# Scores of the second attention in two fp32r passes of stacked halves, with unrotated context keys and queries in four places in turn

## The chip, the cores and the metric

The program runs on one core of a Trainium2 chip, in one launch. The metric is device time in microseconds, the median of several runs. The engines are TensorE (PE; PEld is its loading of weights), VectorE (DVE), ScalarE (ACT), GpSimd (POOL) and SyncE (SP, which here only issues DMAs). Each takes its instructions in the order in which they are written, and they wait for each other by semaphores.

## The reference, cut to what matters

Two layers run over 1024 latent tokens and 256 context tokens of width 1024. The change touches the attention of the second layer (odd_mixer): 12 query heads in 4 groups that share keys and values, width 64, a window of plus and minus 128 tokens beside the whole context, and a learned sink in the softmax.

```python
k_ctx, v_ctx = gqa_keys_values(h_ctx, k_g)            # rmsnorm of keys
q_lat = apply_rope(gqa_queries(h_lat, q_g), cos, sin)
k_lat = apply_rope(k_lat, cos, sin)
...
s_ctx = jnp.einsum('bqkgd,bckd->bkgqc', qi, k_ctx).astype(jnp.float32) * scale
s_win = jnp.einsum('bqkgd,bskd->bkgqs', qi, ki).astype(jnp.float32) * scale
s_win = jnp.where(valid, s_win, NEG_INF)
p = jax.nn.softmax(jnp.concatenate([s_ctx, s_win, sink_col], axis=-1), axis=-1)
```

Context keys have no position, so they are normalized but not rotated; in the kernel before they go through the rotation all the same, with a table that leaves them as they are.

## The kernel before

The stage is heads1(), one block between the projection of queries, keys and values and the output projection. QK1 holds for each group G two tiles of 128 rows: tile 0 has the queries of head j = 2 and the keys, tile 1 the queries of heads j = 0 and 1. Columns 0 to 1023 are latent tokens, 1024 to 1279 context.

Preparing a group takes five **products** w = 0 to 4 (prods): tile 0 in chunks of 512, 512 and 256 columns (c = 2 is the context keys), tile 1 in two of 512. A product goes through ACT's square, PE's norms (one matmul with bones for the sum of squares into bank NB, one with rot1 into bank TB), ACT's inverse (Ln, Exp), and on DVE turn (L2060, q times cos and gain, into t1) and rotated (L2074, L2077, and the multiplications of L2084 that write qa and ka, 64 rows each; semaphore "out"). POOL's cast makes bf16 copies qb and kb of them.

The bf16 copies serve the **maxima**: for each head jj = 0, 1, 2 of a group (j = 2, 0, 1) and query tile qt, PE's maximum (L1908 to L1913) makes scores in banks RB and RB + 1, and DVE's reduce_max (L2095) their largest; the next maximum on PE waits until the one before it is reduced ("mc"). After eight of them DVE's negated and PE's rows (L1923) put the negative maxima in one row, and ACT's row (L1983) copies it to row 64 of qa, where ka has a one, so that the QK matmul subtracts it. The next maximum waits for that copy ("mr").

A **head** n has six pairs u of score units, two of context (512 queries each) and four of window tiles (256 or 384 queries). PE's qk (L1844, fp32, and masks at L1847) makes the units in three banks in turn, ACT's attend (L2005) takes the exponential, PE's pv (L1855) multiplies by values, POOL's add (L1812, L1817) sums the probabilities. For the head before, PE's spread (L1876, L1880) brings sum and sink to all rows in bank NB, in pair u = 1; ACT's inverse_sum (L2012, L2014) inverts, DVE's finish (L2050) writes the output in pair u = 2. ACT's end copies the head's output (L2021) and takes the sink's exponential (L2023).

The order on each engine is written out by hand. A **pair** is a step of 0 to 71 (6 per head, NP_ = 18 per group). In each, PE does qk of the next pair, spread if u = 1, the steps of side 0, pv, the steps of side 1; ACT does the exponentials of the next pair, inverse_sum, then its steps; DVE finish and its steps; POOL casts and add. slots says which steps stand where: product() puts one at pair o + r, o the group's first pair, r = -15, -13, -9, -7, -3, and maxima() starts at r = -8, -2 and 4. What group 0 needs before its first head has the pair UPFRONT; it makes the setup, before the first qk. Banks NB and TB are shared by norms and spread: spread waits for "out" of the norms issued so far, norms for "out" of the product before.

## Time and profile before

| | |
|---|---|
| median of 3 runs | 3388.43 us (3385.56 to 3391.74) |
| the profiled execution's own time | 3388.43 us |
| its span | 3386.7 us |
| PE busy | 3165.7 us (93%) |
| DVE, ACT, POOL busy | 1582.6, 1015.1, 464.9 us |
| heads1, from its start to its last copies | about 2215 to 2533 us |
| QK matmuls of the stage | 288 records, two for each fp32 matmul |

Busy time is summed over an engine's instructions; PE's ends are modelled, so the distance of two starts says more about the cost of a piece than its length. A row of a timeline merges equal neighbours (x4 is four of them), and what stands in brackets is the engine's idle time before it and who ended it.

### The profile page before, as it was taken

How to read it: one execution, taken by the hardware profiler on the slowest of the kernel's cores; microseconds unless marked ns; L12 is line 12 of the kernel's file. 1: busy time of each engine (PE TensorE's matmuls, PEld its weight loads, DVE VectorE, ACT ScalarE, POOL GpSimd, SP SyncE). 2: the span in 40 equal slices, each digit the busy share in tenths (PEclk: the TensorE clock that was granted, in tenths of full speed). 3: DMA queues.
4: the chain of work that ended last, by engine and by line, in shares of the span. 5: the costliest groups of instructions: out<-in, count | busy, mean ns of one | idle time of the engine just before them, and what ended most of it. 6: DMA issues, size and time to landing. Idle time of an engine off the chain costs nothing. (4 is left out here: it accounts for less than half of the span.)

```text
span 3386.7 us, 37587 instructions
## 1 busy us (share of the span) xinstructions
PE 3165.7 (93%) x14242; PEld 2176.1 (64%) x14242; DVE 1582.6 (47%) x1955; ACT 1015.1 (30%) x1363; POOL 464.9 (14%) x367
## 2 busy tenths in 40 slices
PE   5987999999897999999999978879989899999998
PEld 2552333333386888888888856734438688888887
DVE  4123544554425454444444553355533555555554
ACT  3014555555413111111111131025542312221221
POOL 0002555555400000000000000035540000000000
PEclk8987999999998999999999989989999999999999
DMA  9800000000201111111111001000001211111111
GB/s 381 326 36 17 4 3 2 3 3 0 85 27 46 37 37 37 37 37 37 37 37 37 31 13 44 31 16 1 1 13 37 70 44 43 62 43 40 47 62 50
DMA packets 34911, 162.27 MB, mean 48 GB/s; under 512 B 3890, under 2 KB 6706, under 8 KB 24755
## 3 DMA queue, kind: packets, MB, share of 16 engines
q1 hardware_dynamic: 34834, 161.24, 13.3%
q8 instruction: 49, 0.80, 0.1%
q14 instruction: 28, 0.22, 0.0%
HBM read 157.03 MB, written 4.19 MB: 48 GB/s over the span
## 5 line engine op out<-in xcount | busy, mean ns | idle before, releaser
L716 PE MATMUL PS<-f_uh,f_Wh 128*128 128x512 f32 (+1 forms) x1760 | 483.4, 372 | 26.0 <-DVE f_ul L453 25.2
L716 PE MATMUL PS<-f_ul,f_Wh 128*128 128x512 f32 (+1 forms) x1760 | 481.4, 371 | 0.0
L716 PE MATMUL PS<-f_uh,f_Wl 128*128 128x512 f32 (+1 forms) x1760 | 481.3, 371 | 0.0
L866 DVE SCALAR_TENSOR_TENSOR X<-PS,mod,X 128x512 f32<-128x512 f32 (+1 forms) x440 | 305.9, 697 | 308.2 <-PE PS L716 308.2
L716 PEld LDWEIGHTS PS<-f_uh,f_Wh 128*128 128x128 f32 x1760 | 308.2, 188 | 89.6 <-issue 19.4
L716 PE MATMUL PS<-f_gh,f_WDh 128*128 128x512 f32 (+1 forms) x880 | 330.4, 375 | 19.5 <-DVE f_gl L852 17.2
L716 PEld LDWEIGHTS PS<-f_ul,f_Wh 128*128 128x128 f32 x1760 | 308.5, 188 | 59.1
L716 PEld LDWEIGHTS PS<-f_uh,f_Wl 128*128 128x128 f32 x1760 | 308.3, 188 | 59.1
L716 PE MATMUL PS<-f_gl,f_WDh 128*128 128x512 f32 (+1 forms) x880 | 325.3, 370 | 0.0
L716 PE MATMUL PS<-f_gh,f_WDl 128*128 128x512 f32 (+1 forms) x880 | 324.6, 369 | 0.0
L835 DVE SCALAR_TENSOR_TENSOR part<-PS,part,part 128x1023 f32<-128x1023 f32 (+1 forms) x132 | 130.0, 1012 | 329.9 <-ACT part L771 329.9
L771 ACT ACTIVATE part<-PS,part 128x1280 f32<-128x1280 f32 (+1 forms) x88 | 115.7, 1315 | 420.6 <-PE PS L716 420.6
L1214 POOL TENSOR_TENSOR X<-X 128x1024 f32<-128x1024 f32 x96 | 227.9, 2374 | 78.1 <-ACT X L1429 78.1
L777 ACT ACTIVATE part<-part 128x1280 f32<-128x1280 f32 (+1 forms) x44 | 51.4, 1169 | 621.0 <-DVE part L841 621.0
L1239 PE MATMUL PS<-part,part 97*128 97x512 f32 x480 | 232.9, 608 | 0.7 <-ACT part L1420 0.7
L716 PEld LDWEIGHTS PS<-f_gh,f_WDh 128*128 128x128 f32 x880 | 166.1, 189 | 54.3 <-issue 17.9
L1429 ACT ACTIVATE X<-PS 128x512 f32<-128x512 f32 x252 | 146.1, 593 | 179.7 <-PE PS L1239 154.1
L716 PEld LDWEIGHTS PS<-f_gl,f_WDh 128*128 128x128 f32 x880 | 166.4, 189 | 27.9
L716 PEld LDWEIGHTS PS<-f_gh,f_WDl 128*128 128x128 f32 x880 | 166.3, 189 | 28.1
L1785 POOL MEMSET part<- 64x1280 f32 x2 | 2.3, 1161 | 1310.8 <-POOLq L134 1310.8
L1528 DVE TENSOR_REDUCE part<-PS 128x1 f32<-128x512 f32 (+1 forms) x312 | 162.9, 580 | 30.2 <-PE PS L1325 29.0
L823 DVE TENSOR_TENSOR f_Wl<-part,f_Wh 128x1024 fp32r<-128x1024 f32 x88 | 107.5, 1222 | 105.6 <-ACT f_Wh L761 105.6
(255 smaller groups left out, 4283.0 us busy)
## 6 DMA issues: line engine op xcount, KB each, us to landing
part<-in_mod_w SPq DMA_DIRECT2D x48, 1024.0 KB, 7.4
part<-in_w_up SPq DMA_DIRECT2D x88, 512.0 KB, 3.5
part<-in_w_down SPq DMA_DIRECT2D x22, 1024.0 KB, 5.6
part<-in_w_out SPq DMA_DIRECT2D x16, 512.0 KB, 3.5
X<-in_xT SPq DMA_DIRECT2D x4, 1280.0 KB, 9.8
X<-in_xT SPq DMA_DIRECT2D x1, 5120.0 KB, 16.1
part<-in_wqk SPq DMA_DIRECT2D x8, 512.0 KB, 3.5
out<-X SPq DMA_DIRECT2D x16, 256.0 KB, 2.0
```

Of the source, the lines that this page charges most:

```text
L716: mm = pe.matmul(ps(bank + c, hi - lo), w_, x_[:, lo:hi], start=f_, stop=l_)
L771: act.activation((cg, cv)[kind][:, :], psv(UPB[kind]), ACT.Identity, scale=cw[:, ds(f, 1), 1], bias=cw[:, ds(f, 1), 3]).then_inc(s["cen"], 1)
L777: act.activation(sg[:, :], cg[:, :], ACT.Silu).then_inc(s["silu"], 1)
L823: dve.tensor_tensor(Wl[place % 2][:, :, :], W[place % 2][:, :, :], Wh[place % 2][:, :, :].bitcast(F32), ALU.subtract).then_inc(s["lo"], 1)
L835: op = dve.scalar_tensor_tensor(out=x[:, lo + 1:hi], in0=h[:, lo:hi - 1], scalar=cw[:, ds(f, 1), 0], in1=x[:, lo + 1:hi], op0=ALU.mult, op ...
L866: dve.scalar_tensor_tensor(out=X[:, m, lo:hi], in0=ps(DNB[r % 2], hi - lo), scalar=moda(layer, 5, m, 0 if lo < SEQ else 1), in1=X[:, m, lo ...
L1214: op = pool.tensor_tensor(ac[:, 0:SEQ], ac[:, 0:SEQ], p[:, :], ALU.add)
L1239: mm = pe.matmul(ps(i % 3, BANK), ka[b][0:97, u * P:(u + 1) * P], qa[b][0:97, n * BANK:(n + 1) * BANK], start=True, stop=True)
L1429: act.activation(pr[u % 3][:, i % 2 * BANK:i % 2 * BANK + BANK], ps(i % 3, BANK), ACT.Exp, scale=A_SCALE).then_inc(s["P"], 1)
L1528: dve.reduce_max(mc[:, r:r + 1], ps(RB + c, hi - lo), AX_X).then_inc(s["mc"], 1)
L1785: pool.memset(ka[b][64:P, :], 0.0).then_inc(s["zero"], 1)
```

## The change

Queries and keys get fp32r tiles. qh holds the high half of a query (rounded to fp32r) in rows 0 to 63 and again in rows 64 to 127, ql the low half (the value less the high half) in rows 0 to 63, with the row of maxima in row 64 and the sink's exponential in row 96. ks holds the low half of a key in rows 0 to 63 and the high half in rows 64 to 127, kh the high half and the row of ones. A unit of QK is two matmuls into one bank: ks with qh, and kh with ql.

The product ends in t1 (one multiplication of 128 rows); a new step "hi" on ACT (high) copies t1 to the high places, and a new step "lo" on DVE (low) subtracts. Both stand one pair after the rotation, POOL's cast waits for "hi", and t1 is free for the next product after "lo". Context keys (c = 2) have neither turn nor rot matmul. Queries have four places in turn, by head, in place of two sets of three. The products stand at r = -15, -13, -12, -6, -3, and the upfront ones are interleaved (upfront). The table of the rotation comes in two loads without its context columns, and PE no longer waits for it; es, osb, lnr and sq lie elsewhere.

```diff
@@ -1681,22 +1681,28 @@
...
-                return big(part[0] - n, *shape)
-            qa = [[take(SEQ) for _ in range(C_GROUP)] for _ in range(2)]
-            ka = [take(T) for _ in range(2)]
-            pr = [take(2, BANK) for _ in range(3)]
-            osb = take(BANK)
-            acc = [take(SEQ) for _ in range(2)]
-            rope = take(2, T)
-            qb = [take(SEQ // 2).bitcast(BF16) for _ in range(C_GROUP)]
-            kb = [take(T // 2).bitcast(BF16) for _ in range(2)]
...
+                return part[0] - n
+
+            def halves(kind, n, size):
+
+                return [place(f"h1_{kind}{b}", take(size), size) for b in range(n)]
+
+            def plain(*shape):
+                return big(take(*shape), *shape)
+
+            QS = 4
+            qh, ql = halves("qh", QS, SEQ), halves("ql", QS, SEQ)
+            ks, kh = halves("ks", 2, T), halves("kh", 2, T)
...
+            rope = [plain(SEQ), MIX1[:, 5, :]]
...
+            sq = [QK1[:, 4 * b + 1:4 * b + 4:2, SEQ:T] for b in range(2)]
+            t1, lnb, osb, lnr = [X[:, 2 * b:2 * b + 2, SEQ:T] for b in range(4)]
...
@@ -1720,9 +1726,18 @@
...
                 at(pair - 1, 1 if pair > 1 else 0, "sq", G, w)
+                at(pair - 1, 1 if pair > 1 else 0, "tn", G, w)
                 at(pair, 0, "nt", G, w)
                 at(pair, 1, "ro", G, w)
+                at(pair + 1, 0, "hi", G, w)
                 at(pair + 1, 0, "ca", G, w)
+                at(pair + 1, 1, "lo", G, w)
...
+            def upfront(n):
...
+                for kind, w in [("sq", 0), ("nt", 0)] + [(kind, w + d) for w in range(n) for kind, d in (
+                        ("sq", 1), ("tn", 0), ("ro", 0), ("nt", 1), ("hi", 0), ("lo", 0), ("ca", 0)) if w + d < n]:
+                    at(UPFRONT, 0, kind, 0, w)
...
@@ -1735,8 +1750,12 @@
             def plan(G):
 
                 o = NP_ * G
-                for w, r in enumerate((-15, -13, -9, -7, -3)):
-                    product(o + r if G else 1 if w == 4 else UPFRONT - 1, G, w)
+                if G == 0:
+                    upfront(NW - 1)
+                    product(1, G, NW - 1)
+                else:
+                    for w, r in enumerate((-15, -13, -12, -6, -3)):
+                        product(o + r, G, w)
...
@@ -1769,6 +1788,21 @@
...
+                def queries(G, j):
+
+                    return (C_GROUP * G + JS.index(j)) % QS
+
+                def operands(G, w):
+
+                    t_, c = prods[w]
+                    b, lo, hi = G % 2, *CH[c]
+                    j = 2 if t_ == 0 else 0
+                    low, high = slice(0, 64), slice(64, P)
+                    out = [] if c == 2 else [(low, qh[queries(G, j)], low, high, ql[queries(G, j)])]
+                    if t_ == 0:
+                        return out + [(high, ks[b], high, None, kh[b])]
+                    return out + [(high, qh[queries(G, 1)], high, low, ql[queries(G, 1)])]
+
                 def halved(x, m):
                     return x[:, 0:m // CTX, :]
 
@@ -1777,31 +1811,31 @@
...
-                    sp.dma_start(rope, a["rope1"]).then_inc(s["tab"], 16)
+                    for t_ in range(2):
+                        sp.dma_start(rope[t_], a["rope1"][:, t_, 0:SEQ]).then_inc(s["tab"], 16)
...
-                        pool.wait_ge(s["out"], NW * G + w + 1)
+                        pool.wait_ge(s["hi"], NW * G + w + 1)
                         at_least(pool, "mx", 24 * (G - 1) + (8 if t_ == 0 else 24))
                         if t_ == 0:
                             if c < 2:
-                                pool.tensor_copy(qb[2][0:64, lo:hi], qa[b][2][0:64, lo:hi])
-                            op = pool.tensor_copy(kb[b][0:64, lo:hi], ka[b][0:64, lo:hi])
+                                pool.tensor_copy(qb[2][0:64, lo:hi], qh[queries(G, 2)][0:64, lo:hi].bitcast(F32))
+                            op = pool.tensor_copy(kb[b][0:64, lo:hi], kh[b][0:64, lo:hi].bitcast(F32))
                         else:
-                            pool.tensor_copy(qb[0][0:64, lo:hi], qa[b][0][0:64, lo:hi])
-                            op = pool.tensor_copy(qb[1][0:64, lo:hi], qa[b][1][0:64, lo:hi])
+                            for j in range(2):
+                                op = pool.tensor_copy(qb[j][0:64, lo:hi], qh[queries(G, j)][0:64, lo:hi].bitcast(F32))
                         op.then_inc(s["cast"], 1)
...
@@ -1839,10 +1873,14 @@
                             at_least(pe, "P", i - 2)
                             if u == 0 and c == 0:
                                 pe.wait_ge(s["mr"], n + 1)
+                                pe.wait_ge(s["lo"], NW * G + (3 if j == 2 else NW))
...
-                            mm = pe.matmul(ps(i % 3, w), ka[G % 2][:, kt * P:(kt + 1) * P],
-                                           qa[G % 2][j][:, q0 * P:q1 * P], start=True, stop=not last)
+                            q = queries(G, j)
+                            pe.matmul(ps(i % 3, w), ks[G % 2][:, kt * P:(kt + 1) * P], qh[q][:, q0 * P:q1 * P],
+                                      start=True, stop=False)
+                            mm = pe.matmul(ps(i % 3, w), kh[G % 2][:, kt * P:(kt + 1) * P], ql[q][:, q0 * P:q1 * P],
+                                           start=False, stop=not last)
...
@@ -1890,9 +1928,12 @@
...
                         nb, tb = banks(G, w)
-                        pe.matmul(ps(nb, hi - lo), bones, sq[q % 2][:, :hi - lo], start=True, stop=True)
-                        pe.matmul(ps(tb, hi - lo), rot1[:, 1 - t_, :], QK1[:, 2 * G + t_, lo:hi],
-                                  start=True, stop=True).then_inc(s["nt"], 1)
+                        m = hi - lo
+                        mm = pe.matmul(in_halves(ps(nb, m)), bones, halved(sq[q % 2], m), start=True, stop=True)
+                        if c < 2:
+                            mm = pe.matmul(ps(tb, m), rot1[:, 1 - t_, :], QK1[:, 2 * G + t_, lo:hi],
+                                           start=True, stop=True)
+                        mm.then_inc(s["nt"], 1)
...
@@ -1976,12 +2016,27 @@
...
+                    def high(G, w):
...
+                        act.wait_ge(s["out"], q + 1)
...
+                        for rows_, first, own, other, second in operands(G, w):
+                            x = halved(t1[rows_], m)
+                            act.activation(in_halves(first[own, lo:hi]), x, ACT.Copy)
+                            if other:
+                                op = act.activation(in_halves(first[other, lo:hi]), x, ACT.Copy)
+                            else:
+                                op = act.activation(in_halves(second[0:64, lo:hi]), x, ACT.Copy)
+                        op.then_inc(s["hi"], 1)
...
@@ -2056,34 +2114,48 @@
...
-                        at_least(dve, "out", NW * G + w)
+                        if c == 2:
+                            return
+                        at_least(dve, "lo", NW * G + w)
...
-                                                 in1=in_halves(rope[:, 0, lo:hi]), op0=ALU.mult, op1=ALU.mult)\
+                                                 in1=in_halves(rope[0][:, lo:hi]), op0=ALU.mult, op1=ALU.mult)\
...
                     def rotated(G, w):
-                        b = G % 2
...
                         q = NW * G + w
+                        r = (NW - 1) * G + w - (w > 2)
+                        nb, tb = banks(G, w)
+                        norm_ = in_halves(ps(nb, m))
+                        if c == 2:
+                            at_least(dve, "lo", q)
+                            dve.wait_ge(s["rinv"], q + 1)
+                            dve.scalar_tensor_tensor(out=halved(t1, m), in0=in_halves(QK1[:, 2 * G + t_, lo:hi]),
...
+                            return
...
-                        dve.tensor_tensor(T_, T_, rope[:, 1, lo:hi], ALU.mult).then_inc(s["ts"], 1)
-                        dve.wait_ge(s["ts"], q + 1)
-                        dve.wait_ge(s["t1"], q + 1)
+                        dve.tensor_tensor(T_, T_, rope[1][:, lo:hi], ALU.mult).then_inc(s["ts"], 1)
+                        dve.wait_ge(s["ts"], r + 1)
+                        dve.wait_ge(s["t1"], r + 1)
                         dve.tensor_tensor(halved(t1, m), halved(t1, m), in_halves(T_), ALU.add).then_inc(s["ta"], 1)
-                        dve.wait_ge(s["ta"], q + 1)
+                        dve.wait_ge(s["ta"], r + 1)
                         dve.wait_ge(s["rinv"], q + 1)
-                        dsts = [qa[b][2] if c < 2 else None, ka[b]] if t_ == 0 else [qa[b][0], qa[b][1]]
-                        for r, dst in enumerate(dsts):
-                            if dst is not None:
-                                rows_ = slice(64 * r, 64 * r + 64)
-                                op = dve.tensor_tensor(in_halves(dst[0:64, lo:hi]), halved(t1[rows_], m),
-                                                       in_halves(ps(nb, m, rows_)), ALU.mult)
-                        op.then_inc(s["out"], 1)
+                        dve.tensor_tensor(halved(t1, m), halved(t1, m), norm_, ALU.mult).then_inc(s["out"], 1)
...
+                    def low(G, w):
...
+                        dve.wait_ge(s["hi"], NW * G + w + 1)
+                        for rows_, first, own, other, second in operands(G, w):
+                            out = second[0:64, lo:hi] if other else first[0:64, lo:hi]
+                            op = dve.tensor_tensor(in_halves(out), halved(t1[rows_], m),
+                                                   in_halves(first[own, lo:hi].bitcast(F32)), ALU.subtract)
+                        op.then_inc(s["lo"], 1)
...
```

## Rows read from the trace of the kernel before

**Rows 1.** The page: span, and busy time of each engine.

```profile
span 3386.7 us, 37587 instructions
...
PE 3165.7 (93%) x14242; PEld 2176.1 (64%) x14242; DVE 1582.6 (47%) x1955; ACT 1015.1 (30%) x1363; POOL 464.9 (14%) x367
```

**Rows 2.** Busy time by stretch, engine by engine, with granted clock (PEclk).

```profile
2214.90:2249.80 34.90, 18.53 (x54) 7.80 (x54) 23.26 (x35) 7.80 (x13) 14.48 (x17) 0.66 0.11 38
2249.80:2533.00 283.20, 273.89 (x1370) 124.17 (x1370) 146.04 (x198) 145.07 (x251) 136.37 (x137) 0.99 0.00 1
```

**Rows 3.** Timeline of ACT: Ln of product 2, groups two apart.

```profile
2297.11 0.47 ACT L1973 ACTIVATE X<-PS,eps 128x256 f32<-128x256 f32 x1 [0.43 <-PE PS L1894]
...
2439.13 0.47 ACT L1973 ACTIVATE X<-PS,eps 128x256 f32<-128x256 f32 x1 [0.43 <-PE PS L1894]
```

**Rows 4.** Timeline of PE: start, length, engine, line, operation, tiles, shape, count.

```profile
2301.65 1.94 PE L1844 MATMUL PS<-part,part 128*128 128x512 f32 x4
2303.43 1.02 PE L1893 MATMUL PS<-part,cst 128*128 128x512 f32 x2
...
2305.14 0.27 PE L1908 MATMUL PS<-part,part 128*128 128x256 bf16 x1
...
2314.31 1.08 PE L1855 MATMUL PS<-part,part 128*64 128x512 f32 x4
2315.34 0.27 PE L1908 MATMUL PS<-part,part 128*128 128x256 bf16 x1
...
2315.72 0.86 PE L1844 MATMUL PS<-part,part 128*128 128x384 f32 x2
```

**Rows 5.** Timeline of the projection before heads1, on fp32r operands.

```profile
2082.17 0.63 PE L555 MATMUL PS<-u1h,qk_wh 128*128 128x512 f32 x2
...
2082.64 0.63 PE L555 MATMUL PS<-u1l,qk_wh 128*128 128x512 f32 x2
```

**Rows 6.** Groups by line and shape: count, busy us, mean ns, idle before.

```profile
L2095 DVE TENSOR_REDUCE part<-PS 128x1 f32<-128x640 f32 x72 | 59.1, 824 | 76.8 <-PE PS L1913 76.7
...
L2005 ACT ACTIVATE part<-PS 128x384 f32<-128x384 f32 x72 | 35.4, 491 | 44.7 <-PE PS L1847 43.4 <-POOL part L1817 1.1
...
L2084 DVE TENSOR_TENSOR part<-X,PS 64x512 f32<-64x512 f32 x32 | 21.9, 684 | 1.1 <-DVE X L2077 0.4
...
L2023 ACT ACTIVATE part<-part,sml 1x1024 f32<-1x1024 f32 x12 | 13.7, 1143 | 0.3
...
L1973 ACT ACTIVATE X<-PS,eps 128x512 f32<-128x512 f32 x16 | 11.0, 688 | 34.0 <-PE PS L1894 34.0
...
L1963 ACT ACTIVATE part<-part 128x512 f32<-128x512 f32 x16 | 9.9, 621 | 5.4 <-PEq L134 5.4
```

**Rows 7.** Timeline of the setup: memsets, first norms, first reductions, first QK.

```profile
2215.14 2.89 DVE L2117 MEMSET part<- 64x640 uint32 x5 [1.26 <-PEq L134]
...
2220.48 2.07 PE L1893 MATMUL PS<-part,cst 128*128 128x512 f32 x2 [7.92 <-DMA part<-in_rope]
...
2224.30 0.70 DVE L2074 TENSOR_TENSOR PS<-PS,part 128x512 f32<-128x512 f32 x1 [3.01 <-PE PS L1894]
...
2241.09 2.97 DVE L2095 TENSOR_REDUCE part<-PS 128x1 f32<-128x512 f32 x4
...
2249.85 5.37 PE L1844 MATMUL PS<-part,part 128*128 128x512 f32 x8 [1.20 <-ACT part L1983]
```

**Rows 8.** L2060 (min/median/max ns), and one of it beside POOL's adds.

```profile
L2060 DVE SCALAR_TENSOR_TENSOR X<-part,sml,part x20: 485/777/1498, 2220.5 to 2460.9; 128x512 f32<-128x512 f32 x16, 128x256 f32<-128x256 f32 x4
...
2300.02 3.54 POOL L1817 TENSOR_TENSOR part<-part,part 128x384 f32<-128x384 f32 x3
...
2301.20 1.50 DVE L2060 SCALAR_TENSOR_TENSOR X<-part,sml,part 128x512 f32<-128x512 f32 x1
```

**Rows 9.** Timeline of PE: maximum 4 of head 1 in group 0.

```profile
2265.12 0.28 PE L1908 MATMUL PS<-part,part 128*128 128x256 bf16 x1 [1.76 <-POOL part L1804]
```

**Rows 10.** Busy time of PE and granted clock by stretch, setup.

```profile
2242.00:2246.00 4.00, 3.29 (x20) 0.69 0.00 0
```

More of the change, by code:

```diff
@@ L1753, in heads1 @@
                      ("tab", "one", "zero", "pad", "s8", "S", "P", "PV", "sq", "nt", "ln", "rinv",
-                      "t1", "ts", "ta", "out", "cast", "mx", "mc", "mn", "mrow", "mr", "o", "es",
+                      "t1", "ts", "ta", "out", "hi", "lo", "cast", "mx", "mc", "mn", "mrow", "mr", "o", "es",
                       "ad", "bc", "lnr", "rs", "fin")}
@@ L1784, in _ @@
                     for b in range(2):
[L1785 removed]
+                        pool.memset(kh[b][64:P, :].bitcast(F32), 0.0).then_inc(s["zero"], 1)
                         pool.wait_ge(s["zero"], b + 1)
[L1787 to L1790 removed]
+                        pool.memset(kh[b][64:65, :].bitcast(F32), 1.0).then_inc(s["one"], 1)
+                    for x in ql:
+                        pool.memset(x[64:P, :].bitcast(F32), 0.0).then_inc(s["one"], 1)
                     def cast(G, w):
@@ L1879, in spread @@
                         for c in range(2):
-                            mm = pe.matmul(ps(NB, BANK, slice(64 * c, 64 * c + 64)), ones[64:65, 0:64],
-                                           es[64:65, c * BANK:(c + 1) * BANK], start=False, stop=True)
+                            mm = pe.matmul(ps(NB, BANK, slice(64 * c, 64 * c + 64)), ones[96:97, 0:64],
+                                           ql[n % QS][96:97, c * BANK:(c + 1) * BANK].bitcast(F32), start=False, stop=True)
                         mm.then_inc(s["bc"], 1)
@@ L1991, in side @@
                                 inverse(*what)
+                            elif kind == "hi":
+                                high(*what)
                             elif kind == "row":
@@ L2020, in end @@
                         at_least(act, "fin", n)
-                        act.activation(osb, ps(OB, BANK), ACT.Copy).then_inc(s["o"], 1)
+                        act.activation(osb, in_halves(ps(OB, BANK)), ACT.Copy).then_inc(s["o"], 1)
                         at_least(act, "bc", n)
-                        act.activation(es[64:65, :], qa[G % 2][j][64:65, :], ACT.Exp, scale=C_SCALE,
+                        act.activation(ql[n % QS][96:97, :], ql[n % QS][64:65, :].bitcast(F32), ACT.Exp, scale=C_SCALE,
                                        bias=sml[64:65, W_SINK + h:W_SINK + h + 1]).then_inc(s["es"], 1)
@@ L2110, in side @@
                                 rotated(*what)
+                            elif kind == "lo":
+                                low(*what)
                             elif kind == "max":
```

54 lines of the change are left out of this document (28 added, 26 removed).

## The prediction

> **What bounds the kernel now.** I read the page first: TensorE (PE) is busy 3165.7 of a span of 3386.7 us, so a change counts where it takes PE work away or makes PE wait [rows 1]. The profiled execution's own time is 3388.43 us, 1.7 above its span, and equals the median of the three runs, so the sum below is made against 3388.4. The shown runs lie 6.2 us apart; 0.2% is 6.8 us, about what a measurement can tell from no change.
>
> Then the busy time by stretch, cut at the two borders of heads1. A setup of 34.9 us (2214.9 to 2249.8) runs at a mean granted clock of 0.66 with PE busy half the time; then come 283.2 us in which PE is busy 273.9, at a clock of 0.99, against 146 for DVE, 145 for ACT and 136 for POOL [rows 2]. So the setup is a chain of latencies, and the rest is PE's alone. The row of Ln on 256 columns (once in a group, product 2) comes at 2297.11 and, two groups later, at 2439.13: a group of 18 pairs takes 71.0 us [rows 3]. Inside a pair PE starts its next piece where the last ends. The reader should read the starts, not the durations (the ends are modelled): two QK units of 512 take 1.78 us (2301.65 to 2303.43), a norms step of 512 1.71, a PV 1.03, one maximum 0.38 [rows 4].
>
> **What is taken away: fp32 QK.** A unit of 512 columns costs 1.78/2 = 0.89 us. The new passes run on fp32r operands, which this trace has in the projection before: two matmuls of 512 in 0.47 us (2082.17 to 2082.64), each with its own weights [rows 5]. A unit is now two such passes, 0.47. A head has 4 units of 512, 6 of 384, 2 of 256, in all 4864 columns or 9.5 units of 512; twelve heads, 114. At 0.42 each that is 48 us; part of 0.89 is the edge between instructions, so I take 46. Context keys (c = 2) no longer have the rot matmul: half of 1.71 for 512 columns, so 0.43 for 256, four times, 1.7. Together **-47.5**. Bounds: -44 if the edges stay whole, -48.
>
> **What is added.** Each product now ends in a step "hi" on ACT (four copies of 64x512; two of 64x256 for c = 2) and a step "lo" on DVE (two subtractions; one). The nearest copy of ACT from SBUF takes 0.62 us and, back to back, some 0.53 apart: "hi" is 2.1 us. The nearest DVE row with its shape is the old write of the result, 64x512 at 0.68 [rows 6]; two are 1.4, and one multiplication of 128x512 takes the place of two of 64x512, so DVE's "ro" is 0.7 shorter. But the subtraction has both inputs in SBUF, as the rotation's first operation (L2060) has, and that takes from 0.485 to 1.50 us, 1.50 while POOL runs its adds [rows 8]. POOL's casts now wait for the same "hi" as the subtractions, so they run at the same moment. I take 2.0 us for "lo" (1.4 alone; 2.8 if each is doubled).
> The Trainium skill says, on the page "SBUF — State Buffer", section "Who interferes with whom", that a DVE instruction with two SBUF inputs contends with a GpSimd instruction that reads SBUF and that one holds the other up whole. The spread of L2060 agrees; by the rule an add of 384 columns could hold a subtraction up for all of its own time, and each "lo" would cost more than my 2.0.
>
> In busy time all of this fits: per group ACT gets 4 x 2.1 + 0.8 = 9 us more on 145/4 = 36, DVE nearly the same as before, where PE would have 71.0 - 11.8 = 59. On average nobody replaces PE. The order of the queues is another matter. "hi" stands on ACT between the exponentials; "lo" stands on DVE *before* the reduction of a maximum in two slots of a group, and PE may not issue maximum m + 1 before the reduction of m is done. And spread shares banks with the norms, so it waits for "out" of the last norms issued, and the norms of products 2 and 3 now stand one pair before a spread.
>
> **Stalls in one group**, PE against the chain, pairs counted from the group's first:
> - Pair 13 (product 3). After spread, ACT does the two steps of inverse_sum (1.3, by the Ln and Exp of a product), then "hi" 2.1, DVE "lo" 2.0, then the reduction 0.82; with handovers 6.5. PE meanwhile has maximum 0.38, PV 1.18, maximum 0.38, QK 1.0 = 3.0. It waits **3.5**.
> - Pair 16 (product 4). From the pair's start ACT has 1.1 left, a copy of a row (1x1024, as the sink's row, 1.14), exponentials 1.0 (2 x 0.49) [rows 6], "hi" 2.1, then "lo" 2.0, reduction 0.8: 7.1. PE reaches its next maximum at 4.1 (QK 1.0, two passes of 512 for each of two units, or of 384 with masks; wait for the row copy and maximum 0.8; PV 0.95; maximum 0.38; QK 1.0). **3.0**.
> - Pair 6 (products 1 and 2), before the spread of pair 7. ACT is at Ln and Exp of product 1 until 0.5 us into the pair, then at a square (0.3), the end of the head (copy 0.6, sink 1.1) and the exponentials (1.0) until 3.5; "hi" of product 1 to 5.6; "lo" to 7.7; DVE's last multiplication of product 2 0.6 more, 8.3. PE reaches the spread at 4.5 (QK 0.98, maximum, norms 0.43 with a wait, PV, maximum, QK 0.65). **3.8**.
> - Small ones: spread of pair 13 behind "out" of product 3, 0.95; square of product 1 behind "hi" of product 0, 0.5; norms 2 behind "out" of product 1, 0.5; three row copies against a shorter QK, 1.0.
>
> Sum 13.3 per group. It is more than the 11.8 that QK and rot give back, so a group with products would take 59.2 + 13.3 = 72.5 against 71.0. Three groups have such a cycle (products of groups 1 to 3), 40 us; the first already has about 2 of idle in it. **+38**. Behind the last product 15 pairs run free and keep their gain, less **1** for row copies.
>
> **Setup.** Before, the first norms wait for the table until 2220.48 and are seen at 2224.30 (3.8 us, twice the 1.71 of the fast clock); the reductions start at 2241.09 and QK at 2249.85 [rows 7]. Now PE waits only for the memsets, which end at 2218.0, so the first norms are seen near 2222. But upfront() interleaves, and DVE and ACT are both in order: "lo" 0 waits for "hi" 0, which stands behind Ln and Exp of product 1 (square and norms: 2222 + 1.3 + 0.6 + 3.8 = 2227.7; done 2229.0); "hi" 0 to 2231.2, "lo" to 2233, rotation 1 to 2236, "hi" 1 to 2238.4; the square of product 3 only then, its norms at the low clock to 2243, Ln and Exp to 2244.2, "hi" 2 to 2245, rotation 3 to 2248.6, "hi" 3 to 2250.9, "lo" 3 to 2252.5. The reductions of all eight maxima stand behind it: 2252.5 against 2241.09, **+11.5**. Bounds +8 (clock high for the norms, no contention) and +14.
> - Product 4 of group 0, norms in pair 1: maximum 4 needs its cast, already a wait of 1.76 us on POOL [rows 9]; now "hi" (2.1) and a shorter QK come before it: **+3** (2 to 4).
> - Clock. In the setup, behind idle, PE was granted 0.69 over 2242 to 2246 us though busy 3.29 of the 4, so a good part of it at 1.2 GHz [rows 10]. Waits of 3 us in a stream may bring the same; I take **+3** for nine of them.
> The rest has cover: two smaller loads in place of one, memsets of POOL (four places in place of six), the lower place of t1 and osb.
>
> Sum: -47.5 + 38 + 1 + 11.5 + 3 + 3 = +9; 3388.4 + 9 = **3397 us**.
>
> **Rivals.**
> - *The waits stay hidden* (other side). If "lo" is never in front of a reduction that PE needs, because "hi" starts before the point that I give it, groups run at 59 us: 3388.4 - 47.5 + 11.5 + 3 + 1 = 3356. For it: ACT and DVE are busy only half the time [rows 2]. It decides at the 3.0 us that PE has between spread and the next-but-one maximum: "hi", "lo" and reduction alone are 4.9. Chance 0.19. Half the stalls, 3377: 0.12.
> - *The clock falls in the waits.* Each of nine long waits is followed by a stretch of about 4 us at 1.2 GHz [rows 10], costing some 1.5 to 2 us: 9 x 1.7 = 15 in place of 3: 3409. Against it: with PE busy 82% of a group the clock could stay. Chance 0.17. The Trainium skill (page "TensorE: Matmul & The Clock Gate", section "What's actually happening") has the throttled state as the default that activity releases; that speaks for this rival.
> - *The passes are not at the fp32r rate here* (the change doesn't do what it says): at 0.89 per unit again, the stalls shrink to those of spreads and setup: 3388.4 + 15 + some 10 = 3413. Nothing in rows 5 speaks for it. Chance 0.04.
> - My forecast, stalls that eat the gain, 3390 to 3404: 0.48.
>
> **The numbers.** Slower by over 0.2% (above 3395.2): two thirds of the forecast 0.31, the clock 0.15, the rate 0.04 = 0.50. Same: rest of the forecast and an edge of the clock case, 0.20. Faster: 0.30. The range must go down into the rival of hidden waits: 3364 to 3413 leaves out about 0.15 below and 0.04 above. The likeliest case's own range is 3388 to 3406 (stalls 11 to 16 per group, setup 8 to 14).
>
> **What would show it.** QK passes of 512 about 0.235 us apart; fp32r copies and subtractions on ACT and DVE, 64x512 at 0.6 and 0.7 to 1.3; PE idle in heads1 of some 40 to 50 us, released by DVE's reduction twice a group and by DVE's last product before the spread of pair 7; the group period near 72 us in place of 71.0; first QK some 61 us behind 2200 in place of 49.85. If the group period is near 60, my ledger of the queues is wrong; if the period is 72 with stalls elsewhere, only their places are.

## The result, and the profile after

| | |
|---|---|
| the changed kernel | 3435.77 us, median of 4 runs |
| the kernel before, beside it | 3387.78 us (3385.56 to 3391.74, 4 runs) |
| ratio | 1.0131 [1.0107, 1.0155]: slower by 48 us by the medians, 44 by the ratio |
| profiled execution | 3435.32 us, span 3433.5 us, against 3388.43 and 3386.7 |

One of the four runs, of 4083.2 us, was disturbed; the ratio leaves it out. The other three are 3426.07, 3435.32 and 3436.22 us, so what an experiment gains on the changed kernel is 1 to 4 us more by the medians than by the ratios; where that matters, the stretch of the heads in the two traces is given too. The forecast was 3397 (3364 to 3413): slower is right, by five times the amount. The page has PE busy for 11 us less than before, and still the span is 46.8 us longer [rows 1].

```profile
span 3433.5 us, 37657 instructions
...
PE 3154.6 (92%) x14234; PEld 2177.8 (63%) x14234; DVE 1603.5 (47%) x1963; ACT 1053.4 (31%) x1435; POOL 473.6 (14%) x365
```

Next the windows of the changed kernel, cut at the first memset of POOL, the first QK and the first matmul of the output projection ([rows 2] ended 8 us ahead of that); the last row is one cycle of the groups, from Ln on 256 columns to the next one.

```profile
2215.17:2261.85 46.68, 18.74 (x52) 7.64 (x53) 24.33 (x36) 16.25 (x27) 15.25 (x15) 0.59 0.07 23
2261.85:2586.49 324.64, 260.60 (x1364) 125.02 (x1365) 168.61 (x209) 178.43 (x313) 144.20 (x137) 0.87 0.01 4
2387.19:2469.92 82.73, 67.64 (x354) 32.69 (x354) 47.96 (x59) 47.52 (x84) 38.33 (x36) 0.90 0.00 1
```

The kernel before, with the same cuts:

```profile
2214.95:2249.85 34.90, 18.53 (x54) 7.83 (x55) 23.26 (x35) 7.80 (x13) 14.48 (x17) 0.66 0.11 38
2249.85:2541.38 291.53, 273.90 (x1371) 124.17 (x1371) 149.24 (x202) 148.66 (x255) 136.37 (x137) 0.98 0.01 5
```

The setup is 11.8 us longer, the stretch of the heads 33.1, all the rest 1.9. This cycle takes 82.7 us and the one before it 85.7, where both took 71.0 [rows 3]. PE's granted clock in the heads fell from 0.98 to 0.87. These are PE's waits of over 0.4 us in one cycle, from the timeline:

```profile
2389.47 1.08 PE L1914 MATMUL PS<-part,cst 128*64 128x512 f32 x4 [2.55 <-DVE X L2136]
...
2412.67 1.08 PE L1914 MATMUL PS<-part,cst 128*64 128x512 f32 x4 [0.73 <-DVE X L2148]
...
2423.93 0.37 PE L1949 MATMUL PS<-part,part 128*128 128x256 bf16 x1 [6.12 <-issue]
...
2438.88 0.37 PE L1949 MATMUL PS<-part,part 128*128 128x256 bf16 x1 [3.51 <-issue]
...
2460.88 1.13 PE L1932 MATMUL PS<-part,cst 128*128 128x512 f32 x2 [0.57 <-ACT part L2003]
...
2466.76 0.67 PE L1932 MATMUL PS<-part,cst 128*128 128x256 f32 x2 [1.50 <-issue]
```

They sum to 15.0 us; the ledger had 13.3. The two long ones are the two maxima behind a "lo"; there the view names no releaser ("issue"), so we must look at what DVE did. Around the 6.12, all engines:

```profile
2417.87 0.63 ACT L2031 ACTIVATE h_qh<-X 64x512 fp32r<-64x512 f32 x1
2418.53 4.57 DVE L2156 TENSOR_TENSOR h_ql<-X,h_qh 64x512 fp32r<-64x512 f32 x2 [2.42 <-ACT h_qh L2031]
2418.62 1.62 POOL L1838 CAST part<-h_qh 64x512 bf16<-64x512 f32 x2 [13.32 <-issue]
2420.21 2.33 POOL L1846 TENSOR_TENSOR part<-part,part 128x1024 f32<-128x1024 f32 x1
2422.63 0.87 ACT L2062 ACTIVATE part<-PS 128x384 f32<-128x384 f32 x2 [4.13 <-issue]
...
2423.02 0.81 DVE L2167 TENSOR_REDUCE part<-PS 128x1 f32<-128x640 f32 x1
```

The two subtractions take 4.57 us for both; the forecast had 2.0. They start together with POOL's casts, which were waiting for the same "hi", and run into POOL's add, which had stood ready behind the casts. The add also lets go the exponentials of the next pair, which wait 4.13. Taken one by one, the first subtraction lasts 0.68 us and the second, from 2419.23, 3.87: it ends 0.56 behind the add. By this pair alone the contention could be the whole story; the experiments ask how much of the 48 us it is, how much is the order of the queues, how much the passes and how much the clock.

### The profile page after: what moved, and what is told of

Same layout as the page of the kernel before. It is cut to its first block and busy times, and to the rows that moved or that the text cites. A ratio compares the mean times of both kernels' runs of the same rounds, so it can differ in the third digit from the quotient of the medians.

```text
span 3433.5 us, 37657 instructions
## 1 busy us (share of the span) xinstructions
PE 3154.6 (92%) x14234; PEld 2177.8 (63%) x14234; DVE 1603.5 (47%) x1963; ACT 1053.4 (31%) x1435; POOL 473.6 (14%) x365
## 6 DMA issues: line engine op xcount, KB each, us to landing
X<-in_xT SPq DMA_DIRECT2D x1, 5120.0 KB, 16.1
```

## The experiments

Times are medians, each beside the kernel before on the same chip; the ratio is to that kernel.

**1. One wait moved: POOL's cast behind "lo".** In groups 1 to 3 the casts can no longer run beside the subtractions.

```diff
-                        pool.wait_ge(s["hi"], NW * G + w + 1)
+                        pool.wait_ge(s["lo" if G else "hi"], NW * G + w + 1)
```

> The changed kernel, but POOL's cast of the groups after the first waits for the subtractions (lo) in place of the copies (hi), so that neither the casts nor the add of 1024 columns behind them can run beside the subtractions. Theory 1 (the two subtractions of pair 13 take 4.57 us because POOL's instructions hold them up): they fall to 1.4, the wait of PE in pair 14 falls from 6.12 to about 3.0 us in each of three groups, and with less of the low clock behind it the run gets 9 to 15 us shorter, 3421 to 3427. Rival (the length comes from something else in the subtraction, such as its output type or its two inputs alone): the subtractions stay above 3 us and the time stays within 3 us.

3427.89 us (3426.12 to 3429.65), 1.0113 [1.0096, 1.013]. The same place in this kernel:

```profile
2409.44 1.38 DVE L2156 TENSOR_TENSOR h_ql<-X,h_qh 64x512 fp32r<-64x512 f32 x2 [2.42 <-ACT h_qh L2031]
...
2410.94 1.16 POOL L1838 CAST part<-h_qh 64x512 bf16<-64x512 f32 x2 [13.22 <-issue]
...
2412.07 2.34 POOL L1846 TENSOR_TENSOR part<-part,part 128x1024 f32<-128x1024 f32 x1
...
2414.49 0.87 ACT L2062 ACTIVATE part<-PS 128x384 f32<-128x384 f32 x2 [5.09 <-issue]
```

Nothing but POOL's start is different, and the pair of subtractions is down from 4.57 to 1.38: the contention is shown. The maximum now waits 2.94 instead of 6.12. But POOL's add comes no earlier, the exponentials wait 5.09, and the next QK waits for them. So only 8 us came back (6 by the ratios; the heads take 320.94 against 324.64), less than the 9 to 15 expected.

**2. The other order on DVE: "lo" behind the reductions** of its pair, for products 3 and 4.

```diff
-                at(pair + 1, 1, "lo", G, w)
+                if lo:
+                    at(pair + 1, 1, "lo", G, w)
...
-                        product(o + r, G, w)
+                        product(o + r, G, w, w < 3)
...
+                for w, r in ((3, -6), (4, -3)):
+                    if G:
+                        at(o + r + 1, 1, "lo", G, w)
```

> The changed kernel, but for products 3 and 4 of groups 1 to 3 the subtractions stand on DVE behind the reduction of the maximum in the same slot, not ahead of it. Theory 1 (PE waits in pairs 14 and 17 because that reduction is queued behind the subtractions): the waits of 6.1 and 3.5 us go, 29 us in three groups; theory 2 (each long wait is followed by a stretch at 1.2 GHz): another 8 to 15 us come back with it, in all 3391 to 3400. If the clock falls for another reason (a group has too little work for PE in any case) only the waits come back, 3405. Rival to both: the wait moves to the next maximum and the time stays above 3420.

3418.07 us (3416.14 to 3421.18), 1.0085 [1.0068, 1.0102]: a miss, by 18 us and more. The maxima no longer wait, and a QK does:

```profile
2334.31 4.56 DVE L2160 TENSOR_TENSOR h_ql<-X,h_qh 64x512 fp32r<-64x512 f32 x2 [0.92 <-ACT h_qh L2035]
2334.39 1.62 POOL L1842 CAST part<-h_qh 64x512 bf16<-64x512 f32 x2 [13.35 <-issue]
2335.98 2.33 POOL L1850 TENSOR_TENSOR part<-part,part 128x1024 f32<-128x1024 f32 x1
2338.40 0.87 ACT L2066 ACTIVATE part<-PS 128x384 f32<-128x384 f32 x2 [4.12 <-issue]
...
2338.94 0.69 PE L1884 MATMUL PS<-h_qh,h_ks 128*128 128x384 f32 x1 [3.76 <-ACT part L2066]
```

POOL has the cast ahead of the add, and sat 13.35 us idle for it, the last 9 with the add's data at hand (ACT's exponentials of that pair end at 2325.17). The expectation had looked at DVE's queue alone; the same product blocks two queues.

**3. The old places** of the products, all else as changed.

```diff
-                    for w, r in enumerate((-15, -13, -12, -6, -3)):
+                    for w, r in enumerate((-15, -13, -9, -7, -3)):
```

> The changed kernel with the products at the places of the kernel before (-15, -13, -9, -7, -3). Theory 1 (spread waits in pairs 7 and 13 because the norms of products 2 and 3 stand one pair ahead of it): the waits of 2.55, 1.50 and 0.73 us before norms 2 and the spreads go, 14 us in three groups, but product 3's subtractions stand in pair 12, behind no spread, so the 6.1 us wait gets shorter too, to some 3: 3405 to 3418. Rival (the waits are set by the amount of work of ACT, whatever the places): within 5 us of 3436.

3433.76 us (3433.23 to 3435.88), 1.0128 [1.0111, 1.0145]: no difference from the changed kernel, as the rival had it, and the expectation is a miss by 16 us. The waits have other places (4.74, 3.50, 2.76, 2.11 for POOL's cast of product 2, 1.23), and a cycle takes 83.4 and 83.9. The new places are not the cause, and do not help either. That the amount of ACT's work sets the waits, as the rival says, is not shown by it: experiment 6 takes the longest of them away with the same work.

**4. The passes alone.** The kernel before, its queries and keys in fp32r tiles and each unit as two fp32r matmuls of the same operands: no low halves, no "hi", no "lo". It leaves out the low half and counts the high one twice.

```diff
-                            mm = pe.matmul(ps(i % 3, w), ka[G % 2][:, kt * P:(kt + 1) * P],
-                                           qa[G % 2][j][:, q0 * P:q1 * P], start=True, stop=not last)
+                            for f_ in (True, False):
+                                mm = pe.matmul(ps(i % 3, w), ka[G % 2][:, kt * P:(kt + 1) * P],
+                                               qa[G % 2][j][:, q0 * P:q1 * P], start=f_, stop=not (f_ or last))
```

> The kernel before with one edit: qa and ka are fp32r tiles, and a QK unit is two fp32r matmuls of the same two operands in place of one in fp32; the scores come out doubled and there is no low half. No step of the halves on ACT or DVE. It prices the passes alone. Forecast: 44 to 48 us shorter than the kernel before, 3340 to 3344, if PE stays what the stage waits for. Rival (the other engines' chains at once take up what PE gives, even without the halves): less than 30 us shorter, above 3358.

3355.26 us (3353.66 to 3359.35), 0.9898 [0.9882, 0.9915]. That is 34.4 us less than before, a gain, but smaller than both 46 and the expectation. The timeline of the changed kernel shows one part of why; a pair of units there:

```profile
2320.32 0.48 PE L1880 MATMUL PS<-h_qh,h_ks 128*128 128x512 f32 x1
2320.64 0.39 PE L1882 MATMUL PS<-h_ql,h_kh 128*128 128x512 f32 x1
2320.87 0.40 PE L1880 MATMUL PS<-h_qh,h_ks 128*128 128x512 f32 x1
2321.11 0.39 PE L1882 MATMUL PS<-h_ql,h_kh 128*128 128x512 f32 x1
2321.48 0.27 PE L1949 MATMUL PS<-part,part 128*128 128x256 bf16 x1
```

Inside the run a pass takes the 0.23 to 0.24 that was forecast. The first takes 0.32, and behind the last the next maximum starts 0.37 later: 1.16 for the pair of units, where 0.94 was counted (1.03 where an fp32 matmul follows). Pairs of 384 with their masks take 1.21 to 1.26 (2317.44 to 2318.70, for one), where 1.63 less 0.63 was counted, 1.00. The pairs of experiment 4 take the same times. Set against the kernel before, with the same neighbours, a pair of 512 is 0.6 to 0.8 us shorter, where 0.84 was counted, and a pair of 384 is 0.40 to 0.57 shorter, where 0.63 was. Over 24 pairs of 512, 36 of 384 and 12 of 256 that makes some 39 of the 48 us. The other part is waits: in the heads of experiment 4 PE is busy 36.7 us less and waits 5.4 us more. The stretch of the projection from which the price came [rows 5] is one long run, without such edges.

**5. The casts one pair later**, behind "lo" (all but product 2's, which keeps its place).

```diff
-                at(pair + 1, 0, "ca", G, w)
+                at(pair + (2 if G and w != 2 else 1), 0, "ca", G, w)
...
-                        pool.wait_ge(s["hi"], NW * G + w + 1)
+                        pool.wait_ge(s["lo" if G and w != 2 else "hi"], NW * G + w + 1)
```

> The changed kernel with POOL's casts of groups 1 to 3 one pair later (two pairs behind the norms, but product 2's at its old pair) and behind the subtractions. In the changed kernel the cast of pair 13 stands on POOL before the add of that pair and waits for the copies (hi), so the add of 1024 columns ends 4.1 us after ACT is ready for the next exponentials, and it runs beside the subtractions. Theory 1 (POOL's queue and the lock with DVE make the wait of pair 14): subtractions 1.4 us unless an add meets them, PE's wait in pair 14 at most 3 us, ACT's wait for POOL there gone; 3418 to 3424, a few us better than the run in which the cast waits for the subtractions in its old place (3427.9). Rival (that wait is DVE's queue alone): within 3 us of 3427.9.

3418.27 us (3416.55 to 3421.56), 1.0086 [1.007, 1.0103]. As expected: the QK waits of experiment 1 are gone, the maxima still wait up to 2.94 and 2.64.

**6. Both edits**: 5 and 2 together.

> The same, and the subtractions of products 3 and 4 behind the reduction in their slot. Both causes of the waits in pairs 14 and 17 are away, so these waits (6.1 and 3.5 us in three groups) should be gone and not return as waits for exponentials, as they did in part in the run with the reductions alone (3.76 us behind ACT, which was behind POOL). What is left are the waits before norms 2 and the spreads, 4.8 us a group. Forecast 3395 to 3404. Rival (ACT is too full in any order, so PE waits elsewhere): above 3410.

3393.83 us (3389.85 to 3399.3, 10 runs), 1.0018 [1.0009, 1.0028]. That is 1 us below the expected range. Each edit alone gave 17 to 18 us, the two give 42 (in the heads of the traces 16.4, 13.0 and 39.1): with either one the other queue still held PE up. The longest wait left in a cycle is 2.75, of the spread for DVE's last step of product 2.

**7. New places** on top of 6: products 2 and 3 elsewhere, away from that spread.

```diff
-                    for w, r in enumerate((-15, -13, -12, -6, -3)):
+                    for w, r in enumerate((-15, -13, -10, -7, -3)):
```

> The same, with the products at -15, -13, -10, -7, -3: product 2 three pairs and product 3 two pairs ahead of a spread. The waits before norms 2 and the spreads go too, 4.8 us a group and what the clock gives back: 3378 to 3390, that is about the kernel before, because the setup (+12 us) and the larger wait for the first group's cast (+2.5) stay. Rival: as above, above 3395.

3375.93 us (3371.01 to 3381.83, 8 runs), 0.9967 [0.9955, 0.9979]: 2 us below the expected range, and faster than the kernel before by 12 us, with the whole change in it. Its windows, cut as above:

```profile
2213.04:2259.64 46.60, 18.67 (x52) 7.64 (x53) 24.32 (x36) 16.24 (x27) 15.24 (x15) 0.59 0.07 23
2259.64:2527.29 267.65, 238.24 (x1364) 116.86 (x1365) 153.55 (x209) 176.73 (x313) 139.03 (x137) 0.96 0.02 5
2369.75:2434.64 64.89, 61.25 (x356) 29.95 (x358) 43.16 (x59) 46.88 (x85) 35.96 (x36) 1.00 0.00 1
```

The reader should compare PE's busy time: the same 1364 matmuls took 260.60 us in the changed kernel and take 238.24 here. The work is the same; the clock is not (0.87 and 0.96, and in the cycle 0.90 and 1.00). This puts a price of 22.4 us on the clock, 6.4 of it in each cycle. The waits of this cycle are 0.57, 0.77, 1.02 and 0.41. Its subtractions, by form, against those of the changed kernel's cycle in the fence behind it:

```profile
L2160 DVE TENSOR_TENSOR h_ql<-X,h_qh 64x512 fp32r<-64x512 f32 x6 | 4.1, 684 | 3.6 <-ACT h_kh L2037 1.8 <-ACT h_qh L2035 1.8
```

```profile
L2156 DVE TENSOR_TENSOR h_ql<-X,h_qh 64x512 fp32r<-64x512 f32 x6 | 8.2, 1360 | 5.2 <-ACT h_qh L2031 4.5 <-ACT h_kh L2033 0.5
```

**8. The clock by itself.** The changed kernel, with matmuls that nobody reads put into the two long waits of groups 1 to 3: five of fp32 ahead of the maximum of pair 14, three ahead of that of pair 17. DVE, ACT and POOL keep their order and their contention.

```diff
                     def maximum(G, jj, qt):
                         pe.wait_ge(s["cast"], NW * G + (3 if jj == 0 else 4 if qt < 4 else 5))
+                        if G and (jj, qt) == (0, 7):
+                            fill(5)
+                        if G and (jj, qt) == (1, 2):
+                            fill(3)
```

> The changed kernel, with matmuls that nobody reads (fp32, 512 columns, into bank TB) put on PE where it waits: five before maximum 7 of head 0 (pair 14), three before maximum 2 of head 1 (pair 17), in groups 1 to 3. They take 4.3 and 2.6 us of waits of 6.1 and 3.5 us, so they cost nothing if the waits stay. Theory 2 (the waits let the granted clock fall, and PE then works at 1.2 GHz for some us while there is work): the granted clock stays at 1.00 behind both waits and the run gets 8 to 14 us shorter, 3422 to 3428. Rival (the low clock has another cause, or costs nothing because PE waits again later): within 3 us of 3436, or longer.

3422.99 us (3419.07 to 3426.61), 1.0103 [1.0086, 1.0121]: more work for PE, and 13 us less by the medians (9.5 by the two ratios; 9.4 in the heads by the traces, 315.24 against 324.64). The granted clock behind the wait of pair 14, in windows of 2 us, first of the changed kernel:

```profile
2417.00:2419.00 2.00, 0.81 (x7) 0.48 (x6) 0.47 (x1) 1.48 (x3) 0.38 (x1) 1.00 0.00 0
2419.00:2421.00 2.00, 0.00 (x0) 0.00 (x0) 1.99 (x2) 0.00 (x0) 2.00 (x3) 1.00 0.00 0
2421.00:2423.00 2.00, 0.00 (x0) 0.00 (x0) 2.00 (x1) 0.37 (x1) 1.86 (x2) 0.68 0.00 0
2423.00:2425.00 2.00, 1.07 (x5) 0.58 (x7) 1.96 (x4) 1.13 (x3) 1.78 (x3) 0.50 0.00 0
2425.00:2427.00 2.00, 2.00 (x9) 1.09 (x6) 1.94 (x3) 0.03 (x1) 1.63 (x2) 0.50 0.00 0
2427.00:2429.00 2.00, 2.00 (x6) 0.96 (x6) 0.40 (x2) 0.95 (x2) 0.00 (x0) 0.61 0.00 0
2429.00:2431.00 2.00, 2.00 (x12) 0.63 (x11) 0.90 (x2) 0.90 (x2) 0.00 (x0) 1.00 0.00 0
```

and of the kernel with the filler, whose maximum comes at 2419.74:

```profile
2419.00:2421.00 2.00, 1.84 (x11) 0.71 (x9) 1.96 (x3) 0.98 (x2) 1.78 (x3) 1.00 0.00 0
2421.00:2423.00 2.00, 2.00 (x11) 1.13 (x10) 1.94 (x3) 0.94 (x2) 1.49 (x2) 1.00 0.04 8
2423.00:2425.00 2.00, 2.00 (x14) 0.62 (x12) 1.44 (x4) 1.18 (x2) 0.00 (x0) 1.00 0.01 4
```

Behind the idle wait the clock is at its lower level, 1.2 GHz (0.50), until past 2427; behind the filled one it stays at 2.4 GHz. Six filled waits gave 9.4 us, about 1.6 each. Not every low stretch went: in group 1 the maximum of pair 14 still waited 1.73 us behind its filler, and the clock was low again from 2339 to past 2342; in the cycle shown it was at 0.50 over 2412 to 2414, ahead of the filler and behind the spread's wait of 0.74.

The two long waits are not the only ones with a slow stretch behind them. In the changed kernel the spreads of pair 7 wait 2.00 us in the first of the three groups and 2.55 in the others, and behind each PE works without a pause at the lower level:

```profile
2305.50:2312.00 6.50, 6.50 (x18) 1.34 (x19) 0.82 (x1) 2.03 (x4) 0.74 (x2) 0.51 0.00 0
2391.50:2397.50 6.00, 6.00 (x23) 2.73 (x22) 2.64 (x4) 2.52 (x5) 3.14 (x3) 0.50 0.00 0
2473.50:2479.50 6.00, 6.00 (x18) 1.88 (x18) 1.27 (x2) 2.03 (x4) 1.84 (x2) 0.50 0.00 0
```

Half of that time, 3 us each and 9 in all, is what the lower level costs there, by an estimate from these rows. By the same estimate the low stretches behind the six long waits cost 14 us, of which the filler gave 9.4 back.

**9. The setup by itself.** The changed kernel, with the steps of the first group written out in another order and a second rotation buffer for its products 1 and 3.

```diff
-                for kind, w in [("sq", 0), ("nt", 0)] + [(kind, w + d) for w in range(n) for kind, d in (
-                        ("sq", 1), ("tn", 0), ("ro", 0), ("nt", 1), ("hi", 0), ("lo", 0), ("ca", 0)) if w + d < n]:
-                    at(UPFRONT, 0, kind, 0, w)
+                for step in ("sq0 nt0 sq1 tn0 ro0 tn1 hi0 nt1 lo0 ca0 ro1 sq2 nt2 sq3 ro2 hi1 lo1 ca1 tn3 hi2 lo2 ca2 "
+                             "nt3 ro3 hi3 lo3 ca3").split():
+                    at(UPFRONT, 0, step[:2], 0, int(step[2]))
```

> The changed kernel with the first group's preparation written out anew: the two heads' chains are taken further apart so that products 2 and 3 are not cast before products 0 and 1 have their halves, and products 1 and 3 of that group have a second rotation buffer. Nothing else moves. Theory (the time to the first score is a term of its own, worth its length once): the first score, now at 2261.85, comes some 10 us earlier, near 2251 to 2252, the groups stay at 82 to 86 us, and the whole takes 3424 to 3427. Rival (the early start is lost again in group 0, whose casts come no earlier, or in a lower clock): the first score comes early, but the time stays above 3431.

3424.48 us (3423.59 to 3424.96), 1.0107 [1.009, 1.0124]: 11.3 us less. The setup takes 37.19 us in place of 46.68, and the heads 324.86 in place of 324.64. The new order and the second buffer came together; which of them gave the 9.5 us was not tried.

**10. The setup in the better version**: 7 and 9 together.

> The version with casts one pair later, the low half behind the maxima and places -15, -13, -10, -7, -3 (3375.9 us, first score at 2259.64), with the new order of the first group's preparation as well. Theory: the two gains add, since one lies ahead of the first score and the other in the groups: 3363 to 3368. Rival: with TensorE waiting little in the groups, the early start meets group 0's casts sooner and its wait on GpSimd (4.24 us in the changed kernel) grows by as much: 3372 or more.

3371.23 us (3367.26 to 3373.07), 0.9948 [0.9931, 0.9965]. The setup is shorter by the same 9.4 us, the time by 4.7 (6.4 by the ratios), between the two expectations. From the first QK to the norms of product 2 of group 1, 3.3 us more pass than in experiment 7 (47.83 against 44.52). It is not the rival's wait: that is 4.24 in both, and the others differ by 0.03 at most. It is the clock: the same 185 matmuls keep PE busy 39.03 us at a mean clock of 0.84, against 35.75 at 0.89. Why the low clock falls so much longer there (0.71 over 2273 to 2281, where 7 had 1.00 over 2280 to 2286) is open.

**11. Fewer early maxima**, on top of 10: those that need product 4's cast come a pair later.

```diff
-            EARLY = [(0, 0), (0, 1), (1, 0), (1, 1), (2, 0), (2, 1), (3, 0), (4, 0)]
+            EARLY = [(0, 0), (0, 1), (1, 0), (1, 1), (3, 0), (3, 0), (3, 1), (4, 0)]
```

> The same, and of the maxima of the first group those that need product 4's cast come one pair later. Theory: the wait of TensorE on GpSimd's cast (4.24 us at 2276.75 in the changed kernel) goes down by 2 to 4 us, and the time with it, to 3360 to 3364. Rival: the wait comes back one pair later, as a wait for the same cast, and the time stays within 1 us of the version without this edit.

3371.11 us (3369.72 to 3372.42), 0.9949 [0.9932, 0.9965]: no difference. The wait for POOL went from 4.24 to 2.96 us, and the two after it from 0.55 and 0.83 to 1.90 and 2.22: the rival, as far as the view tells, which names no releaser for the last two.

**12. A single pass**: experiment 4 without the second matmul of a unit. The low half's product is left out wholly.

> The kernel before with its scores from a single pass in fp32r instead of two (3355.3 us with two): the high half of the queries alone, the low half's product left out wholly, so this prices one pass and is no version of the kernel. A second pass of the same weights took 0.235 us per 512 columns. Theory (TensorE sets the time and the second passes cost what they last): 114 of them take 26.8 us, so 3327 to 3332. Rival (other engines have become the bound of the groups by then, at 62.5 us): the gain stays under 15 us, so 3340 or more, and new waits on VectorE or ScalarE stand ahead of the scores.

3348.14 us (3346.03 to 3350.86), 0.9884 [0.9867, 0.99]. Half of QK's columns are gone, and it is 7 us, not 27 (9.7 in the heads of the traces, where PE is busy 22.6 us less and waits 13.0 more). Cycles of 4 and of this kernel:

```profile
2355.38:2418.08 62.70, 60.63 (x358) 30.16 (x360) 41.30 (x58) 36.86 (x66) 34.91 (x36) 1.00 0.00 1
```

```profile
2354.15:2414.16 60.01, 54.41 (x322) 25.26 (x324) 40.48 (x58) 36.43 (x66) 34.86 (x36) 1.00 0.00 1
```

PE works 6.2 us less and waits 3.5 us more in a cycle, though DVE, ACT and POOL are busy two thirds of it at most. The new waits stand ahead of the maxima, not of the scores, and the view names no releaser for them. That a cycle of this order is bound near 60 us by its chains from one engine to the next is read from this, not tried. The gain of faster passes was, by the times, nearly used up at two.

## Why the prediction was right or wrong

The table sets the terms of the sum against what the profiled executions measured. The terms of the heads go from the kernel before over experiment 4, which has the passes and nothing else, to the changed kernel: the stretch takes 291.53, 260.18 and 324.64 us, of which PE is busy 273.90, 237.16 and 260.60.

| term | forecast | measured | from |
|---|---|---|---|
| passes and rot | -47.5 | -31.4 | 260.18 less 291.53 (without rot) |
| waits in the heads, the cast's and the row copies among them | +38 + 3 + 1 | +41.0 | not busy: 64.0 less 23.0 |
| clock | +3 | +23.4 | busy: 260.60 less 237.16; 22.4 against experiment 7 |
| setup | +11.5 | +11.8 | 46.68 less 34.90 |
| outside the stage | 0 | +1.9 | the rest of the span |
| all | +9 | +46.8 | spans 3433.5 and 3386.7 |

- **Passes: direction right, size wrong.** The price of a pass, 0.235, came true inside a run of passes. The step that failed is "I take 46": 2 us were put down for all edges, while every pair of 512 or 384 gives 0.06 to 0.23 less than counted, some 9 us in all. The bound nearer to zero, -44, was still too large. PE was busy 36.7 us less in experiment 4, and 5.4 of it came back there as waits, which the term had at nothing.
- **The ledger of waits: right in sum by luck, wrong in its entries.** 15.0 us in a cycle for 13.3 forecast, and +41.0 in the heads for +42. The wait behind product 3, which shows in pair 14, is 6.12 and not 3.5, by "lo" (4.57 for 2.0) and "hi" (2.53 from 2415.97 to 2418.50, for 2.1). Pair 17 (3.51 for 3.0) and the spread of pair 13 (0.73 for 0.95) are close. Norms 2 wait three times what was put down (1.50 for 0.5). The spread of pair 7 came smaller (2.55 for 3.8), and the row copies (1.0) left no wait over 0.4. The errors cancelled.
- **"lo" at 2.0.** The range ended at 2.8; it took 4.57 beside casts and add, 2.25 beside the casts of product 4, and 1.38 where neither ran beside it. The text had said in so many words that casts and subtractions run at the same moment, and then took a value near the middle. The Trainium skill, page "SBUF — State Buffer", section "Who interferes with whom", says that a DVE instruction with two inputs in SBUF contends with a GpSimd instruction that reads SBUF, and that the port pair they share is locked by one of them at a time. The trace agrees: the second subtraction lasts 3.87 us and ends 0.56 behind POOL's add (2.33).
- **What the ledger lacked**: POOL's own queue. The casts wait for "hi", the add of the pair before stands behind them, and the exponentials wait for the add. In the changed kernel this hides behind the maximum's wait; experiment 2 brought it out.
- **The clock: the rival, and larger.** The forecast took +3, its rival 15 for nine long waits at 1.7 us each. Experiment 8 measures 1.6 per filled wait, near the rival's 1.7; but nine waits of it are 14, and the heads lost 22.4. The rest lies behind the third kind of the nine, the spread of pair 7: at least 9 us by the rows in experiment 8. So the rival had the right nine places, and too low a price for a third of them. Experiment 7, which has no wait over 1.02 in a cycle, has none of these stretches; experiment 6, with the spread's wait still at 2.75, has two (from 2369.5 and from 2441.5, over 6 us each). "With PE busy 82% of a group the clock could stay" is refuted: the cycle is busy for 67.64 of 82.73 us and was granted 0.90. The Trainium skill, page "TensorE: Matmul & The Clock Gate", section "What's actually happening", has the throttled state as the default; the rows of experiment 8 agree.
- **Setup: right**, in size and place: 11.8 for 11.5, first QK at 2261.85 for "some 61", reductions at 2253.03 for 2252.5. Experiment 9 shows that it is worth its length, and that another order with a second buffer takes 9.5 of it away.
- **Hidden waits, the rival of the other side,** did not come, but experiments 5 to 7 show what it takes: the casts behind "lo", "lo" behind the reductions, and product 2 away from the spread. Then a cycle is 64.9 us, near the 62.7 of the passes alone.

So the step that made the forecast fail is twofold: of the 37.8 us between +9 and +46.8, the clock has 20.4 and the passes 16.1; the ledger of waits, on which most of the working went, was right within a microsecond in its sum, though not in its entries.

## What to carry to other kernels

Price a short matmul pass with its edges: take it from a stretch that has as few passes in a row as the place where it goes. When two engines wait for the same event, look at what both then read, and at what is queued behind each of them; move the less urgent one a step later, and put the step that nobody needs yet behind the one that PE waits for. In a stream of matmuls count a wait of TensorE of some us twice, once for its length and once for the slower clock behind it: here nine waits of 2.00 to 6.12 us cost 1.5 to 3.5 us each on top of their length, by the estimate of experiment 8.

## What the runs showed of the hardware that was not expected

- Two subtractions of 64x512, both inputs in SBUF, took 1.38 us with POOL idle, and 4.56 to 4.57 us when POOL's casts and an add ran beside them; the first of the two kept its 0.68 us, the second took 3.87.
- Filling TensorE's waits with matmuls that nobody reads made the kernel faster, by 9.4 us in the heads of the traces and 13 by the medians: behind the wait of pair 14 the clock stayed at 2.4 GHz, where without them it was at 1.2 GHz from before 2423 until past 2427.
- A cycle with waits up to 1.02 us had a granted clock of 1.00 throughout; waits of 2.55, 3.51 and 6.12 us in the changed kernel were each followed by a stretch at 0.50. The length of the wait alone does not decide it: in experiment 8 a wait of 0.74 was followed by such a stretch (2412 to 2414), and in the single-pass kernel one wait of 1.69 of three was (0.50 over 2304.5 to 2310.5).
- Leaving out one of two fp32r passes of QK gave 7 us (9.7 in the heads of the traces) of the 27 that the pass lasts.
